# A two-layer hybrid decoder step on one core: mixer steps cut finer and placed by a table of engine loads, and the HGRN levels as 64-row matmuls

## What is computed

```python
u = _rmsnorm(h, w['norm1_g']) @ w['w_in']          # 1024 -> 25 blocks of 128 columns
y_a = _rglru(...)      # causal conv, gates, linear recurrence
y_b = _swa_prompt(...) / _swa_sample(...)          # window attention, decode with a key/value cache
y_c = _hgrn2(...)      # gated state, chunks
y_d = _mlstm(...)      # matrix state with stabiliser, chunks
h = h + jnp.concatenate([y_a, y_b, y_c, y_d], axis=-1) @ w['w_out']
f = _rmsnorm(h, w['norm2_g']) @ w['w_up']
h = h + jnp.square(jax.nn.relu(f)) @ w['w_down']
h = h + jax.nn.sigmoid(h @ w['w_ple_gate']) * (p_l @ w['w_ple_proj'])
```

## Time and profile before

| what | value |
|---|---|
| median of 3 runs | 3253.83 us (3250.94 to 3255.21) |
| profiled execution, time | 3251.4 us |
| its span | 3249.6 us |
| PE busy | 2919.4 us (90%) |
| POOL, DVE, ACT busy | 1445.2, 1292.8, 1211.0 us |
| mean granted clock of TensorE | 0.950 |

### The profile page before, as it was taken

One profiled execution on the slowest core, in us unless ns is written; L12 is line 12 of the kernel. 1 busy time (PEld: TensorE's weight loads), 2 busy tenths in 40 slices (PEclk: granted clock), 3 DMA queues, 4 the chain that ended last, 5 costly groups with the idle time before them and its releaser, 6 DMA issues.

```text
span 3249.6 us, 43084 instructions
## 1 busy us (share of the span) xinstructions
PE 2919.4 (90%) x18120; PEld 2543.7 (78%) x18120; DVE 1292.8 (40%) x2223; ACT 1211.0 (37%) x1890; POOL 1445.2 (44%) x904
## 2 busy tenths in 40 slices
PE   6898986778999999877999999878798999999998
PEld 5677874566768787677899988766676887999998
DVE  4557245357342243555422243536735112322223
ACT  5652445322332444623332344533233233422233
POOL 4345432245445553344444545224543555454454
PEclk9999997888999999988999999889899999999999
DMA  3211122121122222211122322222122223222232
GB/s 133 78 66 46 59 97 69 60 78 46 61 80 91 97 88 81 72 40 46 59 80 92 99 81 85 66 67 83 39 69 68 95 94 114 98 93 92 91 98 85
DMA packets 77136, 254.86 MB, mean 78 GB/s; under 512 B 10258, under 2 KB 11794, under 8 KB 76944
## 3 DMA queue, kind: packets, MB, share of 16 engines
q1 hardware_dynamic: 66704, 234.39, 22.0%
q10 hardware_dynamic: 10240, 17.72, 1.6%
HBM read 242.77 MB, written 9.31 MB: 78 GB/s over the span
## 4 chain that ended last, share of the span: by engine, by line
PE 69%; DVE 17%; ACT 6%; DMA 3%; issue 3%; POOL 1%; ACTq 0%; DVEq 0%; SPq 0%; POOLq 0%
PE pj L563 20%; PE pj L565 19%; PE pj L564 19%; DVE q_diag L1515 4%; DVE slots L1515 3%; PE pm L808 2%; PE pj L583 2%; DMA slots<-in_vc 2%; DMA w_raw<-in_w 1%; DVE att L1955 1%; DVE lev L1515 1%; ACT w_hi L946 1%; POOL w_raw_r L1399 1%; PE pm L905 1%; PE pm L900 1%
## 5 line engine op out<-in xcount | busy, mean ns | idle before, releaser
L1399 POOL TENSOR_TENSOR w_raw_r<-w_raw,w_hi 128x1024 fp32r<-128x1024 f32 x428 | 1036.8, 2424 | 1407.0 <-ACT w_hi L946 1406.9
L563 PE MATMUL pj<-xop_r,w_hi 128*128 128x260 f32 (+1 forms) x2920 | 942.6, 323 | 24.8 <-DVE xop_r L1540 17.8
L565 PE MATMUL pj<-xop_r,w_raw_r 128*128 128x260 f32 (+1 forms) x2920 | 928.9, 318 | 0.0
L564 PE MATMUL pj<-xop_r,w_hi 128*128 128x260 f32 (+1 forms) x2920 | 928.3, 318 | 0.0
L946 ACT ACTIVATE w_hi<-w_raw 128x1024 fp32r<-128x1024 f32 x428 | 452.3, 1057 | 758.4 <-DMA w_raw<-in_w 743.0
L563 PE MATMUL pj<-ff_r,w_hi 128*128 128x260 f32 (+1 forms) x1664 | 555.1, 334 | 65.7 <-DVE res L1515 34.8
L563 PEld LDWEIGHTS pj<-xop_r,w_hi 128*128 128x128 f32 x2920 | 558.0, 191 | 68.8 <-issue 11.1
L564 PEld LDWEIGHTS pj<-xop_r,w_hi 128*128 128x128 f32 x2920 | 558.4, 191 | 38.9 <-issue 1.7
L565 PEld LDWEIGHTS pj<-xop_r,w_raw_r 128*128 128x128 f32 x2920 | 558.1, 191 | 38.8
L564 PE MATMUL pj<-ff_r,w_hi 128*128 128x260 f32 (+1 forms) x1680 | 551.4, 328 | 0.0
L565 PE MATMUL pj<-ff_r,w_raw_r 128*128 128x260 f32 (+1 forms) x1664 | 544.4, 327 | 0.0
(11 more groups left out here) (415 smaller groups left out, 3104.6 us busy)
## 6 DMA issues: line engine op xcount, KB each, us to landing
w_raw<-in_w SPq DMA_DIRECT2D x428, 512.0 KB, 3.3
res<-in_x SPq DMA_DIRECT2D x8, 520.0 KB, 8.7
res<-in_x SPq DMA_DIRECT2D x8, 512.0 KB, 5.2
out_y<-res ACTq DMA_DIRECT2D x8, 260.0 KB, 3.1
out_y<-res ACTq DMA_DIRECT2D x8, 256.0 KB, 4.4
slots<-in_rope ACTq DMA_DIRECT2D x2, 520.0 KB, 4.2
ff<-in_p ACTq DMA_DIRECT2D x2, 520.0 KB, 3.9
out_kc<-slots ACTq DMA_DIRECT2D x2, 512.0 KB, 3.1
```

Source lines behind the costliest of these rows:

```text
L563: pe.matmul(out, wh, hi[:, cols], start=(k == 0), stop=False)
L564: pe.matmul(out, wh, lo[:, cols], start=False, stop=False)
L565: return pe.matmul(out, wl, hi[:, cols], start=False, stop=(k == nk - 1))
L1399: pool.tensor_tensor(w_lo[:, n % NW, :], w_raw[:, n % NW, :], w_hi[:, n % NW, :].bitcast(F32), ALU.subtract).then_inc(lo_made, 1)
```

## The change

1. Steps are cut smaller: `rows` 4 to 7, `conv` 1 to 2, `lru` 1 to 3, `rope` 3 to 5, `hprep` 2 to 3, `sattn` 4 to 5, `hsample` 2 to 4, `msample` 3 to 5; `h0` becomes `h0` (subtractions), `he` (exponentials) and `hm` (products), `h1` becomes `h1` and `h1b`, `hdiag` gets its POOL part apart as `hdm`.
2. `slot_steps` gives way to `place`: a table holds for each step whether PE takes part, which engines must be nearly clear, and what it loads on DVE, ACT and POOL in tenths of a us; each job pays off a share (SPARE). A step waits in the queue while an engine that it needs is behind, or would be filled beyond a limit. What is not placed by the time of the own `out` is forced there.
3. The HGRN levels are 28 matmuls of 64 rows per chunk, two heads in the two halves of the array. `q_diag` and its 12 half products go; the products stay in place in `lev`.
4. `vt` transposes alternate between two PSUM banks; the scaling of an attention chunk moves to the next `attn` step; scratch of `sattn` moves.
5. `proj` runs both halves first and `pg` after them, instead of half and half.

```diff
@@ the order
-    def slot_steps(gap):
-        heavy = light = False
+    def place(kind, upto=None):
+        heavy, force = False, upto is not None
         while queue:
             i, (step, arg, need) = queue[0]
+            if force and i > upto:
+                return
             at = ready.get((i, JOB[need]))
-            if at is None or count - at < gap:
+            if not force and (at is None or count - at < 1):
                 return
-            if light or (heavy and not _light(step, arg)):
-                return
-            light, heavy = _light(step, arg), True
+            pe, needs, *load = LOAD_OF.get((step, arg), LOAD[step])
+            late = (50, 18, 5, 10)[i]
+            limit = 90 if kind == 'win' else 20 if kind == 'out' else 60
+            if not force:
+                if pe and heavy:
+                    return
+                if any(backlog['dap'.index(e)] > late for e in needs):
+                    return
+                if kind == 'out' and load[0] > 5:
+                    return
+                if any(load[n] and backlog[n] and backlog[n] + load[n] > limit for n in range(3)):
+                    return
+            heavy = heavy or pe
+            for n in range(3):
+                backlog[n] += load[n]
             order.append((step, i, arg))
...
+LOAD = dict(
...
+    h0=(0, '', 35, 0, 45), he=(0, 'dp', 0, 27, 0), hm=(0, 'a', 70, 0, 45), h1=(1, 'dp', 25, 5, 0), h1b=(0, '', 25, 0, 0),
...
+SPARE = dict(win=(55, 38, 33), out=(5, 30, 33), up=(42, 33, 20), down=(40, 45, 33), proj=(45, 10, 33), pg=(32, 33, 33))
@@ the list of jobs
-    ple = [[x for h in range(2) for x in [('proj', i, h)] + [('pg', i, 4 * h + m) for m in range(4)]] + [('end', i, 0)]
-           for i in range(INST)]
+    ple = [[('proj', i, 0), ('proj', i, 1)] + [('pg', i, n) for n in range(KT)] + [('end', i, 0)] for i in range(INST)]
@@ PE, h1
-                    el, half = level(l), 1 << l
                     for j in range(2):
-                        if l < 6:
-                            o = pm[:, b + j, :].rearrange("p (h s) -> p h s", h=2)[:, :, at:at + 64]
-                            pe.matmul(o, el[:, j, :], q_diag[:, l, j], start=True, stop=True)
-                            continue
                         for hh in range(2):
                             r = slice(64 * hh, 64 * hh + 64)
-                            pe.matmul(pm[:, b + hh, j * 256 + at:j * 256 + at + 64], el[r, j, :],
-                                      el[r, j, half:], start=True, stop=True)
+                            o = pm[:, b + hh, j * 256 + at:j * 256 + at + 64].rearrange("p (n b) -> p n b", b=1 << l)
+                            el = level(l)[r, j, :]
+                            pe.matmul(o, el, el.rearrange("p (n two b) -> p n two b", two=2, b=1 << l)[:, :, 1, :],
+                                      start=True, stop=True)
@@ DVE, the query products
+            def hm(i, c):
...
                 for g, levels in enumerate(GROUPS):
                     dve.wait_ge(hc_exp, 3 * n + g + 1)
                     for l in levels:
                         e1 = halves(level(l), l)[1]
-                        if l == 6:
-                            last = tt(e1, e1, halves(q, l)[1], ALU.mult)
-                            continue
-                        for hh in range(2):
-                            r = slice(64 * hh, 64 * hh + 64)
-                            last = tt(q_diag[r, l, :, hh, :].rearrange("p j (n b) -> p j n b", b=1 << l),
-                                      halves(level(l)[r], l)[1], halves(q[r], l)[1], ALU.mult)
+                        tt(e1, e1, halves(q, l)[1], ALU.mult)
@@ PE, vt
-                if v:
-                    pe.wait_ge(vt_c, 5 * i + v)
+                if v > 1:
+                    pe.wait_ge(vt_c, 5 * i + v - 1)
```

More of the change, by code:

```diff
@@ L114, in _mixer @@
     if dec:
-        o += [('msample', n, 'do1') for n in range(3)]
+        o += [('msample', n, 'do1') for n in range(1, 5)]
     o += [('mnorm', n, 'do1') for n in range(2)] + [('ysplit', 3, 'do1')]
     return o
-NO_PE = ('lam', 'rows', 'conv', 'gate2', 'lru', 'kv', 'h0', 'ysplit')
-def _light(step, n):
-    return step in NO_PE or (step, n) in (('rope', 0), ('hprep', 0), ('hprep', 1), ('hnorm', 0), ('mnorm', 0))
+LOAD = dict(
+    lam=(0, 'da', 5, 3, 0), vt=(0, '', 0, 6, 0), rows=(0, '', 35, 0, 0), rowt=(1, 'a', 0, 4, 0), conv=(0, 'a', 50, 0, 0),
+    gate=(1, 'd', 0, 30, 0), gate2=(0, '', 0, 40, 0), lru=(0, '', 35, 0, 0), rope=(1, 'da', 26, 0, 0),
+    kv=(0, 'd', 0, 0, 0), attn=(1, 'da', 45, 35, 0), sattn=(1, 'da', 5, 0, 0), hprep=(0, 'a', 30, 0, 0),
+    hdm=(0, 'd', 0, 0, 26), hdiag=(1, 'p', 0, 2, 0), hload=(0, 'd', 0, 3, 0), hsample=(1, 'd', 14, 0, 0),
+    h0=(0, '', 35, 0, 45), he=(0, 'dp', 0, 27, 0), hm=(0, 'a', 70, 0, 45), h1=(1, 'dp', 25, 5, 0), h1b=(0, '', 25, 0, 0),
+    h2=(1, 'da', 15, 5, 0), hnorm=(1, 'a', 15, 28, 28), mprep=(1, '', 0, 30, 0), m1=(1, 'dap', 15, 15, 8),
+    m2=(1, 'dap', 48, 4, 0), msample=(1, 'd', 43, 0, 0), mnorm=(1, 'a', 30, 28, 0), ysplit=(0, 'dp', 0, 13, 28))
@@ L191, in _order @@
                 ready[(x[1], x[2])] = count
+            for n in range(3):
+                backlog[n] = max(0, backlog[n] - SPARE[x[0]][n])
         if (x[0] in jobs and x[2] != (0, 0)) or x[0] == 'n2':
-            slot_steps(1)
+            place(x[0] if x[0] in jobs else 'up')
     assert not queue
@@ L230, in _tables @@
         elif what == 'rope' and a:
-            for n in range(3):
+            for n in (range(3) if a == 1 else (a - 2,)):
                 for t in range(nt):
@@ L785, in hsample @@
                 l = i // 2
-                pe.wait_ge(ss_p if part else ss_v, l + 1)
-                for n in range(2):
-                    last = pe.matmul(pm[:, 2 * part + n, :], blk, smp_half(n, 4), start=True, stop=True)
-                last.then_inc(ss_pt if part else ss_t, 1)
+                if part == 1:
+                    pe.wait_ge(ss_v, l + 1)
+                    for n in range(2):
+                        last = pe.matmul(pm[:, n, :], blk, smp_half(n, 4), start=True, stop=True)
+                    last.then_inc(ss_t, 1)
+                elif part == 3:
+                    pe.wait_ge(ss_p, l + 1)
+                    for n in range(2):
+                        last = pe.matmul(pm[:, 2 + n, :], blk, smp_half(n, 4), start=True, stop=True)
+                    last.then_inc(ss_pt, 1)
             def h1(i, c):
@@ L1081, in proj @@
                     split_r(i, KT - 1)
-                else:
-                    act.wait_ge(p_v, KT * i + 4)
-                for m in range(4):
-                    take('proj', i, 4 * half + m, ple_proj(i, m), ACT.Copy)
+                for m in range(4 * half, 4 * half + 4):
+                    take('proj', i, m, ple_proj(i, m), ACT.Copy)
             def finished(i, n):
@@ L1435, in proj, with hdm @@
                     split_r(i, KT - 1)
-            def hdiag(i, _):
+            def hdm(i, _):
                 pool.wait_ge(hp_v, i + 1)
@@ L1494, in ysplit @@
                                            ALU.subtract).then_inc(y_lo, 1)
-            steps = dict(nf=nf, up=up, down=down, proj=proj, hdiag=hdiag, h0=h0, hnorm=hnorm, m1=m1, ysplit=ysplit)
+            steps = dict(nf=nf, up=up, down=down, proj=proj, hdm=hdm, h0=h0, hm=hm, hnorm=hnorm, m1=m1,
+                         ysplit=ysplit)
             started = False
@@ L2020, in msample @@
                     dve.wait_ge(mp_w, l + 1)
+                    for n in range(2):
+                        taken(dve, 'mprep', i, n)
+                    for name in ('dq0', 'dq1', 'dk0', 'dk1'):
+                        taken(dve, 'win', i, JOB[name])
                     dve.wait_ge(hc_sv, gi(i, NCH))
```

401 lines of the change are left out of this document (219 added, 182 removed).

## The result

The changed kernel takes 3062.58 us (median of 4 runs, 3061.79 to 3063.16) against 3254.52 us: a ratio of 0.941, 95% interval 0.9394 to 0.9426. That is 192 us less, where 231 were forecast; 3020 was predicted, with a range of 2920 to 3150. The profiled execution has a span of 3061.4 us at a mean clock of 0.973.

What follows compares the result with a forecast made beforehand. Long rows on DVE, ACT or POOL ahead of what PE wants next, not engine throughput, were taken as the loss; -128 + 6 - 78 + 8 - 36 - 13 - 10 + 20 = -231 gave 3020 us, range 2920 to 3150.

Steps and rivals of the forecast that it cites:

- HGRN, with the 64-row form: HGRN stretches: shorter DVE rows and evictions between the pieces take away most of 166 us lost, -128; 64-row products, +6.
- `rowt` to `rope`, instances 1 to 3: Gate rows and rotary: 88 us lost before; steps spread over more jobs leave 10 us, so -78.
- the same, instance 0: Gate rows and rotary of instance 0: PE reaches `rowt` some 14 us early, +8, between 0 and +15.
- decode cache: `sattn` waits for the cache load: three or four jobs now lie behind its issue, -36 of 62 us lost.
- `attn`: Attention steps, split by the change: costed at nothing, because DVE is busy for 40%.
- `msample`: `msample` steps: 9.3 us lost in each of two instances, the same cure, -13 of 18.6.
- `proj`: `proj` ahead of all `pg`: 5.4 us lost in the last stretch, the other three together the same, -10.
- new waits and the rest: New waits: `vt` transposes +9, gate rows ahead of `out` +3, HGRN's `hprep` +3, last odd norm +5; +20 in all.
- pair reading: HGRN's `h1`: 64-row passes of two heads run side by side, 28 pairs in 3.1 us against 3.4 before.
- The +47: Rival for the 64-row passes: two heads don't run side by side, +47 for +6, 3061 us; chance 0.07.
- The waits only move: Rival: waits block elsewhere; half of 128 + 78 + 36 stays, 3141 us, case 3080 to 3240; chance 0.20.
- The ring of weights: Slower rival: weight parts come late at some 170 mixer steps, 3360 us at 2 us each; chance 0.06.

## Why the prediction came out as it did

The direction and the range were right; the time is 43 us above the forecast. That it is no further off is in part luck: two terms brought 14 and 7 to 11 us more than forecast, five brought less. Term by term, with what was lost before and after by the prediction's own prices:

| term | forecast | measured |
|---|---|---|
| HGRN, with the 64-row form | -122 | 30 - 166 = -136 |
| `rowt` to `rope`, instances 1 to 3 | -78 | 18 - 88 = -70 |
| the same, instance 0 | +8 | 27 - 14 = +13 |
| decode cache | -36 | 43 - 62 = -19 |
| `attn` | 0 | 90 - 60 = +30 |
| `msample` | -13 | -14 |
| `proj` | -10 | -1 to -5 |
| new waits and the rest | +20 | +9 to +13 |

`attn`, `msample` and `proj` are summed over their jobs from the records of the passes; in instance 0 the `proj` jobs now carry mixer steps, so their part of the term can't be told apart. The last line is what remains of the span's 3061.4 - 3249.6 = -188. No run tries the -70 of `rowt` to `rope` by itself, nor `msample` and `proj`: these are read from the stretches.

**The step that failed** is the sentence "The split `attn` and `conv` I cost at nothing: DVE is busy for 40%". A share of busy time says nothing about a step whose result PE asks for in the same gap. The diff showed that the scaling moved behind `at_e` of the chunk before, and PE's wait for `at_p` did not move; putting the scaling back returned 25 us. The jobs with `attn` lost 30 us more than before. And DVE's free half isn't free at any time: beside POOL its instructions last longer (a product 0.5 to 0.6 us instead of 0.29).

**The cache term was mis-sized.** The prediction took the 26 us of the earlier trace rows as a time that jobs can hide, and three jobs to hide 17 of it. The wait was still 11.8 us on DVE, and the load of 127 rows was itself the cause: cut in two, it needs 7 us and no cover.

**The HGRN term had about the right size, and the runs part its causes.** The prediction priced two causes together: the shorter row, and evictions between subtractions and products. The form alone, in the old order, brings 82 us; its DVE saving there is 130.9 us of products before against 44.6, or 86, so it came back almost one for one. Bringing the three pieces together again costs 20 us of the gain. The rest, some 30 to 40 us, lies in where `h1` and the chains stand; no run parts it further. The price of a whole product was wrong: 0.21 us, from a row of subtractions that ran while POOL was mostly idle. Beside POOL it took 0.5 to 0.6, so a chunk's products went from 8.2 to 3.6 us, some 4.6 less, not 6.

**The gate rows of instance 0.** The prediction says that PE reaches `rowt` some 14 us early there "as it did before". It didn't before: the wait was 2.3 us, and the 14.1 us were instance 1's. Now it is 16.6. The measured +13 lies near the upper end of the term's range of 0 to +15.

**The pair reading held**: `h1` took 3.46 us, and the term of +6 was zero. The passes have 64 columns to stream, not 32: the rows show 64x64. The +47 that the prediction put beside the rule of the Trainium skill ("TensorEngine Tiling (Array Packing)", Instruction Overhead) did not come, as long as two heads stand next to each other. Where they don't, the passes cost the 47 and the clock about as much again, which the prediction did not have.

**The rivals.** "The waits only move" was in part true, in two places: PE's attention wait, and the gate rows, which moved to instance 0. The ring of weights did not starve (6.7 us before, 5.7 after). The forecast's new wait of 5 to 12 us at the `vt` row came as 7.2.

## What to carry to other kernels

Where PE is fed by small rings, look at the rows of instructions that stand ahead of an eviction on its engine, not at that engine's busy share: 70 us more of work on an engine that was 42% busy made the kernel 65 us longer. And price an instruction from a row in which the neighbouring engines do what they will do then: the row of subtractions beside an idle POOL priced the products at less than half. When a step is cut and moved to the next gap, check for every consumer whether it asks in that same gap; the wait that moves is the one that nobody lists. And where a DMA lands several times later than its neighbours of the same size, look at its shape before giving it cover to hide behind.

## What the runs showed that was not expected

- A product over 64 partitions takes DVE about as long as one over 128: 655 and 609 ns on average for 64x128 and 128x128, most of them beside POOL; the shortest of either took some 285.
- The same DVE sum of 128x4 that takes 0.16 us elsewhere took 2.29 us at 617.14. POOL ran a weight's low part from 617.06 to 619.41, and the sum ended at 619.43.
- 56 small passes one after another brought the granted clock down to 0.50 in each of 16 chunks, for 3 to 10 us, although PE never stood in them; the same 56 in pairs left it at 1.00.
- A load of 127 rows ran at 23 to 28 GB/s, and the same data as 112 and 15 rows landed in 7.2 us.
